# Two weight matrices of a transformer kernel stored in DRAM in the order in which their loads read them

## The reference, cut to what matters

```python
# first layer, after its attention
x = x + routed_experts(rmsnorm(x, g_ffn), w_router, ..., w_gate_up, b_gate_up, w_down, b_down)
hp = rmsnorm(x, g_ple)
x = x + sigmoid(hp @ w_ple_gate) * (p_i @ w_ple_proj)        # w_ple_proj: 256 x 1024
# second layer: ffn1, mixer, then
q = (h @ w_q).reshape(B, S, 4, 256)
k, v = split(m @ w_kv, 2, axis=-1)                           # w_kv: 1024 x 2048, m: the normed memory
x = x + softmax(q k^T / 16) v @ w_o                          # then ffn2 and a last rmsnorm
```

## Time and profile before

| | |
|---|---|
| time, median of 3 runs | 1807.71 us (1806.11 to 1808.63) |
| the profiled execution: its own time | 1808.49 us |
| the profiled execution: span, first to last instruction | 1806.4 us |
| mean granted TensorE clock | 0.986 |
| TensorE matmul busy | 1661.4 us, 92% |
| VectorE busy | 682.6 us, 38% |
| ScalarE busy | 549.8 us, 30% |
| read from memory | 544.00 MB, 302 GB/s over the span |
| packets of the DMA engines | 125870 |

### The profile page before, as it was taken

The page is one execution under the profiler, slowest core; times in us unless marked ns, Lnnn a source line. Parts: engine busy times, 40 slices in busy tenths (PEclk is TensorE's granted clock), DMA queues, the critical chain, the costliest instruction groups (busy, mean ns, idle before and its releaser), DMA issues.

```text
span 1806.4 us, 21425 instructions
## 1 busy us (share of the span) xinstructions
PE 1661.4 (92%) x9479; PEld 1073.3 (59%) x9480; DVE 682.6 (38%) x824; ACT 549.8 (30%) x748; POOL 22.1 (1%) x37
## 2 busy tenths in 40 slices
PE   8999899798879999998888888999999999999998
PEld 7777433232325444442323232379998998989996
DVE  5897411021121121120111111167554865566543
ACT  6565200020111111110000011175443666454442
POOL 0000000000000000000000000010000000000000
PEclk9999999899999999999999999999999999999999
DMA  7527699999999999999999999955555423445552
GB/s 252 169 94 249 262 380 429 422 428 427 428 421 417 406 422 407 418 427 428 428 426 428 428 427 424 420 166 187 186 187 186 164 94 119 165 136 176 186 187 93
DMA packets 125870, 546.46 MB, mean 303 GB/s; under 512 B 5632, under 2 KB 73344, under 8 KB 101104
## 3 DMA queue, kind: packets, MB, share of 16 engines
q1 hardware_dynamic: 124448, 540.96, 75.6%
q0 software_dynamic: 1040, 4.00, 0.7%
q10 hardware_dynamic: 288, 0.11, 0.0%
HBM read 544.00 MB, written 1.05 MB: 302 GB/s over the span
## 4 chain that ended last, share of the span: by engine, by line
PE 66%; DMA 26%; DVE 5%; ACT 2%; issue 1%; SPq 0%; DVEq 0%; ACTq 0%
DMA ring<-in_w_down 25%; PE PS L857 10%; PE PS L819 9%; PE PS L1004 6%; PE PS L520 6%; PE PS L521 6%; PE PS L522 6%; PE PS L487 2%; PE PS L489 2%; PE PS L488 2%; PE PS L778 2%; PE PS L868 2%; PE PS L803 1%; DVE ring L1818 1%; PE PS L506 1%; PE PS L508 1%
## 5 line engine op out<-in xcount | busy, mean ns | idle before, releaser
L819 PE MATMUL PS<-ring,work 128*64 128x512 f32 x2048 | 458.2, 599 | 36.4 <-DMA ring<-in_w_gate_up 36.4
L1818 DVE TENSOR_TENSOR ring<-ring,ring 128x2048 fp32r<-128x2048 f32 (+2 forms) x130 | 289.4, 2234 | 312.8 <-ACT ring L1243 312.7
L819 PEld LDWEIGHTS PS<-ring,work 128*64 128x64 f32 x2048 | 142.9, 138 | 332.7 <-issue 254.4
L1243 ACT CAST ring<-ring 128x2048 fp32r<-128x2048 f32 (+2 forms) x131 | 242.6, 1862 | 221.1 <-DMA ring<-in_mem_w_kv 90.7
L857 PE MATMUL PS<-ring,work 128*64 128x512 f32 x1024 | 240.9, 614 | 58.6 <-DMA ring<-in_w_down 41.3
L857 PEld LDWEIGHTS PS<-ring,work 128*64 128x64 f32 x1024 | 76.1, 140 | 209.8 <-issue 171.2
L2212 DVE TENSOR_SCALAR work<-PS 128x512 f32<-128x512 f32 x32 | 22.1, 690 | 335.5 <-PE PS L819 335.5
L520 PE MATMUL PS<-xr,ring 128*128 128x256 f32 x480 | 136.5, 284 | 1.1 <-DVE xr L2282 1.1
L521 PE MATMUL PS<-xr,ring 128*128 128x256 f32 x480 | 135.8, 283 | 0.0
L522 PE MATMUL PS<-xr,ring 128*128 128x256 f32 x480 | 135.8, 283 | 0.0
L1499 ACT ACTIVATE work<-work 128x512 f32<-128x512 f32 x32 | 20.2, 630 | 376.9 <-DVE work L2212 376.9
(11 more groups left out here) (402 smaller groups left out, 2230.3 us busy)
## 6 DMA issues: line engine op xcount, KB each, us to landing
ring<-in_w_gate_up SPq DMA_DIRECT2D x128, 2048.0 KB, 17.9
ring<-in_w_down SPq DMA_DIRECT2D x64, 2048.0 KB, 16.4
ring<-in_ffn_w_gu SPq DMA_DIRECT2D x44, 1024.0 KB, 5.1
ring<-in_w_in SPq DMA_DIRECT2D x28, 1024.0 KB, 5.5
ring<-in_ffn_w_down SPq DMA_DIRECT2D x22, 1024.0 KB, 4.7
ring<-in_w_out SPq DMA_DIRECT2D x8, 1024.0 KB, 5.1
ring<-in_mem_w_kv SPq DMA_DIRECT2D x8, 1024.0 KB, 14.2
ring<-in_w_ple_gate SPq DMA_DIRECT2D x4, 1024.0 KB, 11.0
```

The lines of the kernel that those rows point to most:

```text
L819: t = e.matmul(PS[hf * 64:hf * 64 + 64, bank, :], XG[g % 2][:, 2 * kp + kk, i * 64:(i + 1) * 64], chunks(raw(w), w)[:, kk, c0 + hf * 512:c ...
L1243: e.copy(hi(j), raw(j)).then_inc(*act.now(("hi", j)))
L1818: e.tensor_tensor(lo(j), raw(j), hi(j).bitcast(F32), ALU.subtract).then_inc(*dve.now(("lo", j)))
```

## The change

`mem_w_kv_2` (1024 x 2048) is stored as 8 arrays of 128 x 2048, one for each part: row p of array c holds the 256 columns of part c from row p of each of the 8 row blocks, one behind the other. `w_ple_proj` (256 x 1024) is stored as 4 arrays of 128 x 512 in the same way. The host does this before the launch. The load of a part names that array as its source. The destination in SBUF, the bytes, the order of the loads, their waits and everything that reads the parts are as before.

```diff
+PACKED = ("mem_w_kv_2", "w_ple_proj")
...
-                    if p.expert < 0:
+                    if p.name in PACKED:
+                        src = w[p.c0 // p.n].rearrange("p (k n) -> p k n", k=p.k)
+                    elif p.expert < 0:
                         src = rows(w, p.k0, p.k, p.c0, p.n)
...
+    for n in PACKED:
+        k, c = arrays[n].shape
+        arrays[n] = np.ascontiguousarray(arrays[n].reshape(k // 128, 128, c // 256, 256).transpose(2, 1, 0, 3)).reshape(
+            c // 256, 128, k * 2)
```

## The result

The changed kernel takes 1800.36 us (median of 5 runs, 1798.47 to 1804.88) beside 1807.71 us of the kernel before (1804.07 to 1810.42). The ratio is 0.9965, with a 95% interval from 0.9949 to 0.9981. Two further comparisons on other occasions gave 0.9979 (0.9963 to 0.9995) and 0.9975 (0.9964 to 0.9986). The mean of the three is 0.9973, which is 4.9 us of 1807.7; the three alone give 6.3, 3.8 and 4.5 us.

The account below looks back on a forecast made before the run. The prediction took the expert stage to be bound by DMA transfers near 428 GB/s. Savings of 4.6 + 0.3 = 4.9 us brought the median from 1807.71 to 1802.8 us, range 1799.5 to 1805.5.

Parts of the forecast that it names:

- A: Whole kernel: the summed gain holds, 1802.8 us, own range 1801.5 to 1804.4; chance 0.58.
- The eight loads: Expert stage, `mem_w_kv_2` loads: 8 KB stretches instead of 1 KB save 0.57 us each, 4.6 us in all.
- The other end: Lower gain for the `mem_w_kv_2` loads, from rates of stretches moving alone: 0.38 us a load, 3.0 us in all.
- The four small loads: Expert stage, `w_ple_proj` loads: 2 KB stretches instead of 1 KB save 0.07 us each, 0.3 us in all.
- Issue and split: SyncE's issue of the twelve DMAs and ScalarE's waits for the eight landings: no gain and no loss.
- TensorE follows: Memory-part experts: 31.9 us of transfer against 30.40 us of TensorE work leaves 1.5 us cover, so no saving is cut off.
- Clock drops and empty queues: Expert stage: three drops cost 3.3 us; term set at 0, ends 3.3 us more gain or 1.1 us less.
- C: Gain cut below what can be measured, by the lower price or one more clock drop: 1805.5 us; chance 0.20.
- E: Slower: the clock falls in all eight experts 11 to 18 and empties the queues, 1811.5 us; chance 0.03.
- Rival B: Expert stage: shorter waits also remove the clock drops, bringing back 3.3 us more, 1799.5 us; chance 0.12.
- Rival D: No gain, 1807.7 us: the engines still move the load in 1 KB packets; chance 0.07.
- The prediction's other estimate: About 3 cycles of overhead per packet of 32-byte beats: 0.2 us a load, some 2 us for the whole change.

Follow-up runs that it names:

- after_again: The changed kernel run again with no edit, compared with the kernel before: ratio 0.9979, median 1802.51 us.
- after_third: The changed kernel run a third time with no edit, compared with the kernel before: ratio 0.9975, median 1803.72 us.
- kv_512: The changed kernel with `mem_w_kv_2` stored block by block, 16 blocks a part, read in 512-byte stretches; ratio 1.0032 against the kernel before.
- kv_2k: The changed kernel with `mem_w_kv_2` stored block by block, 4 blocks a part, read in 2 KB stretches; ratio 0.9989 against the kernel before.

## Why the prediction was right

The forecast was 1802.8 us with a range of 1799.5 to 1805.5. Measured were 1800.36, 1802.51 and 1803.72; the mean ratio gives 4.9 us, the forecast sum. That it agrees to the tenth is luck: the single ratios give 3.8 to 6.3 us. The direction, the place and the mechanism were right, and the 11 experts with their 4.6 us carry that better than the times do. One bound in the prediction is wrong: A's own range should begin at 1807.7 - 5.6 = 1802.1 us, not 1801.5. Nothing else rests on it.

1. *The eight loads, 4.6 us.* Held. The windows give 0.54 us a load (32.38 to 31.84), 0.57 was taken; the 11 experts are 4.6 us shorter. The choice between the two prices was what counted. The other end, from 1 KB stretches that move alone at 367 GB/s, would have given 0.38 us, 3.0 for eight. That end also gave the fixed cost of 0.415 us per MB and (1/KB), 6.8 ns a stretch, where the windows of the expert stage show 9. It was used only to scale from 16 to 8 KB, where it erred by 0.01 us a load. Why 1 KB stretches lose less when they move alone is open.
2. *The four small loads, 0.3 us.* By the windows 0.08 us each, as taken; by the times not to be told from nothing.
3. *Issue and split, nothing.* A DMA is issued 51 ns faster, and ScalarE waits 3.8 us less in all; neither shows up anywhere.
4. *TensorE follows.* Held for the most part: 30.40 us of work in 31.84. In one of the three profiles there are rows of 421 to 424 GB/s with no clock drop, which the kernel before did not have. The smaller slack may be the reason; the other two profiles have 426 to 428 in such rows.
5. *Clock drops and empty queues, zero.* Held as a sum, but the price of a drop and its condition did not. In the changed kernel the experts below 427 GB/s cost 31.92 x 28/427 = 2.1, 0.6, 0.2, 0.4 and 0.4 us, 3.7 us together against 3.3 before. The profiles of the changed kernel have two, four and two drops in this stretch, and before had three. The four drop windows of `after_again` run at 408, 419, 417 and 423 GB/s, 3.1 us together; the two of `after_third` at 400 and 409, 3.4 us. So one drop cost from 0.3 to 2.1 us, and the 11 experts took the same time with two as with four. A mean price of 1.1 us times a count, on which the ends of this term and the rivals C and E rest, is not what these runs show. Nor does a wait of 3 us mark a drop: in the three profiles drops also followed waits of 2.12, 2.14, 2.18, 2.22 and 2.95 us, and none followed 2.24 and 2.70.

Rival B fell: the drops stayed. The first wait shrank from 4.25 to 3.80 us and the clock fell in its last two microseconds or right behind it in all three profiles. B would have needed more than shorter waits, as item 5 shows; the queues were filled by another order of use. Rival D fell with the count of packets and with the windows at 427 GB/s. E, which needed a drop in every expert, didn't come near. C can't be excluded for a single comparison, whose interval is 4 to 6 us wide, and of three ratios one (0.9979) lies where "no change" would be read.

The Trainium skill, page "DMA: Bandwidth & Descriptors", section "Specifications", gives line rate from 512 B on. Here it does not hold: with one thirteenth of its bytes in stretches of 512 B a window runs at 412 GB/s, with the same bytes in 8 KB stretches at 427. The prediction's other estimate, 0.2 us a load from a cost of each packet, is under half of the 0.54 us that the windows give.

## What to carry to other kernels

Where a stage is bound by transfers, count the stretches of DRAM, not the bytes alone. Each cost an engine about 9 ns in this kernel, so 1 MB in 1 KB stretches took some 0.56 us over 16 KB ones. Read that price from a window of the stage itself, with and without the short loads, and not from a stage where they move alone. Where TensorE bounds the stage the same edit was worth nothing measurable, even for 69 thousand packets. And don't price a clock drop by its count: ask whether the slower matmuls hold up a slot that the next load needs.

## What was not expected

`kv_512` moves its eight loads in 16384 stretches, yet its page counts 121262 packets, exactly as many as that of `kv_2k` with 4096 stretches:

```profile
DMA packets 121262, 546.46 MB, mean 302 GB/s; under 512 B 5632, under 2 KB 64128, under 8 KB 96496
```

So four stretches of 512 B were recorded as one packet of 2 KB. The windows still differ by 0.8 us (32.95 and 32.15), and 96 more stretches an engine at 9 ns would be 0.86. So the cost goes with the stretches that the load names and not with the packets that the page counts. The issue of these DMAs also took longer:

```profile
L2647 SPq DMA_DIRECT2D ring<-in_mem_w_kv x8: 707/707/857, 515.5 to 752.2; - x8
```

707 ns against 378 for 1 KB, 378 for 2 KB and 328 for 8 KB. The time of issue is not what makes the windows longer: 1 KB and 2 KB have the same, and their windows differ by 0.2 to 0.4 us. At 512 B the engines' share is 1.01 in both rows above, so they were not left waiting for it either.
